# Expert weights over two DMA queues: the second gate/up quad and the down quad of experts 6 to 27 begun by ScalarE

## The reference

```python
def clamped_swiglu(hgu):
    g, u = hgu[..., :D_EXPERT], hgu[..., D_EXPERT:]
    g = jnp.minimum(g, SWIGLU_LIMIT)
    u = jnp.clip(u, -SWIGLU_LIMIT, SWIGLU_LIMIT)
    return (u + 1.0) * (g * jax.nn.sigmoid(SWIGLU_ALPHA * g))
...
    def expert_block(args):
        tok, e = args
        xb = xn[tok]
        hact = clamped_swiglu(xb @ w_gate_up[e] + b_gate_up[e])
        return hact @ w_down[e] + b_down[e]
```

## Time and profile before

| | before |
|---|---|
| median of 3 runs | 1257.85 us (1256.84 to 1258.02) |
| the profiled execution | 1257.53 us |
| its span, from the first to the last instruction | 1255.7 us |
| PE busy | 1183.1 us (94%) |
| DVE busy | 478.8 us (38%) |
| ACT busy | 250.5 us (20%) |
| bytes moved | 461.49 MB, mean 368 GB/s |

### The profile page before, as it was taken

One profiled execution on the slowest core, in us unless ns is written; L12 is line 12 of the kernel. 1 busy time (PEld: TensorE's weight loads), 2 busy tenths in 40 slices (PEclk: granted clock), 3 DMA queues, 4 the chain that ended last, 5 costly groups with the idle time before them and its releaser, 6 DMA issues.

```text
span 1255.7 us, 18113 instructions
## 1 busy us (share of the span) xinstructions
PE 1183.1 (94%) x7504; PEld 612.6 (49%) x7504; DVE 478.8 (38%) x741; ACT 250.5 (20%) x353; POOL 5.4 (0%) x12
## 2 busy tenths in 40 slices
PE   8999999999899999999999989999999999989997
PEld 7999998998533333333333333333333333333332
DVE  6867867654422332222222322222222222222223
ACT  5439544544400000000100010000000000001002
POOL 0000100000000000000000000000000000000000
PEclk9999999999999999999999999999999999999999
DMA  8525647644999999999999999999999999999995
GB/s 329 197 101 201 243 169 268 237 165 185 384 361 428 430 426 435 432 432 428 428 432 433 434 434 433 428 428 432 433 434 434 433 428 428 432 428 428 426 428 230
DMA packets 27341, 461.49 MB, mean 368 GB/s; under 512 B 3216, under 2 KB 3360, under 8 KB 4512
## 3 DMA queue, kind: packets, MB, share of 16 engines
q1 hardware_dynamic: 26784, 460.16, 87.5%
q0 software_dynamic: 224, 0.54, 0.2%
q10 hardware_dynamic: 288, 0.12, 0.0%
HBM read 459.76 MB, written 1.05 MB: 367 GB/s over the span
## 4 chain that ended last, share of the span: by engine, by line
PE 61%; DMA 37%; DVE 1%; issue 1%; ACT 0%; SPq 0%; DVEq 0%; ACTq 0%
DMA late<-in_w_gate_up 36%; PE ps L1370 29%; PE ps L1235 6%; PE ps L1236 6%; PE ps L1237 6%; PE ps L1419 3%; PE ps L1254 2%; PE ps L1255 2%; PE ps L1256 2%; PE ps L1270 2%; PE ps L1393 1%; PE ps L1427 1%; DMA raw<-in_dense 1%; PE ps L1323 1%; PE ps L1303 1%
## 5 line engine op out<-in xcount | busy, mean ns | idle before, releaser
L1370 PE MATMUL ps<-late,s 128*64 128x512 f32 x1224 | 556.4, 598 | 55.2 <-DMA late<-in_w_gate_up 53.9
L1371 PE MATMUL ps<-late,s 128*64 128x512 f32 x1224 | 556.4, 598 | 0.0
L1370 PEld LDWEIGHTS ps<-late,s 128*64 128x64 f32 x1224 | 155.7, 136 | 395.4 <-issue 304.0
L1119 DVE TENSOR_TENSOR res<-res,ps 128x1024 f32<-128x1024 f32 x64 | 78.1, 1221 | 246.2 <-PE ps L1419 238.8
L1235 PE MATMUL ps<-act_hi,whi 128*128 128x256 f32 x576 | 164.2, 285 | 3.5 <-DVE act_lo L776 1.8
L1237 PE MATMUL ps<-act_hi,wlo 128*128 128x256 f32 x576 | 163.7, 284 | 0.0
L1236 PE MATMUL ps<-act_lo,whi 128*128 128x256 f32 x576 | 163.7, 284 | 0.0
L1371 PEld LDWEIGHTS ps<-late,s 128*64 128x64 f32 x1224 | 155.7, 136 | 0.0
L692 ACT ACTIVATE early<-ps 128x512 f32<-128x512 f32 x64 | 34.7, 594 | 551.4 <-PE ps L1371 551.4
L795 DVE TENSOR_TENSOR wlo<-raw,whi 128x2048 fp32r<-128x2048 f32 x47 | 107.3, 2288 | 51.9 <-ACT whi L525 51.8
L1371 PE MATMUL ps<-raw,s 128*64 128x512 f32 x272 | 123.9, 598 | 0.0
(11 more groups left out here) (195 smaller groups left out, 876.9 us busy)
## 6 DMA issues: line engine op xcount, KB each, us to landing
late<-in_w_gate_up SPq DMA_DIRECT2D x44, 4096.0 KB, 21.0
late<-in_w_gate_up SPq DMA_DIRECT2D x31, 2048.0 KB, 15.7
raw<-in_dense SPq DMA_DIRECT2D x51, 1024.0 KB, 4.8
late<-in_w_down SPq DMA_DIRECT2D x11, 4096.0 KB, 20.6
raw<-in_w_down SPq DMA_DIRECT2D x11, 4096.0 KB, 20.6
late<-in_w_down SPq DMA_DIRECT2D x12, 2048.0 KB, 17.9
raw<-in_w_down SPq DMA_DIRECT2D x7, 2048.0 KB, 20.4
early<-in_w_gate_up SPq DMA_DIRECT2D x5, 2048.0 KB, 9.3
```

The lines of the kernel that those rows point to most:

```text
L1119: V.tensor_tensor(res[:, t, :], res[:, t, :], ps[:, OUT_BANK[t]:OUT_BANK[t] + 2, :].rearrange("p b n -> p (b n)"), ALU.add)\
L1370: nc.tensor.matmul(ps[0:SLOTS, bank, :], x_tile, lower, start=start, stop=stop)
L1371: return nc.tensor.matmul(ps[SLOTS:P, bank, :], x_tile, upper, start=start, stop=stop)
```

## The change

SP keeps the first gate/up quad of each expert from 6 to 27. The second gate/up quad and the down quad are begun by ACT on its own queue. The second quad of e+1 is begun after ACT's two copies of the gate/up rows in the step of e, the down quad of e at the start of ACT's work in the step of e, ahead of the copy of the down rows. The counts of `chunk_used` that are waited for are the same as on SP. ACT's loop over the experts is cut in three (1 to 5, 6 to 27 by twos, 28 to 31), with a branch that leaves out the second quad after expert 27. Before expert 6 and from expert 28 on, all weights stay on SP's queue.

```diff
-            def load_gate_up_quad(e, q):
-                sp.dma_start(flat[QUADS[q]], gate_rows(e, q)).then_inc(filled[QUADS[q]], 16)
...
-            def load_down_quad(i, half):
-                at = QUADS[2 + half]
-                sp.dma_start(flat[at], down_rows(i * 2 + half)).then_inc(filled[at], 16)
...
-                def next_gate_up_quads(e):
-                    for q in range(2):
-                        used(r, e, 4 * q + 3)
-                        load_gate_up_quad(e + 1, q)
-
-                with sp.Fori(QUAD_FROM // 2 - 1, QUAD_UNTIL // 2 - 1) as i:
-                    for half in range(2):
-                        e = i * 2 + (1 + half)
-                        next_gate_up_quads(e)
-                        used(r, e, PER_EXPERT - 1)
-                        load_down_quad(i + 1, half)
+                with sp.Fori(QUAD_FROM - 1, QUAD_UNTIL - 1) as e:
+                    used(r, e, 3)
+                    sp.dma_start(flat[QUADS[0]], gate_rows(e + 1, 0)).then_inc(filled[QUADS[0]], 16)
                 next_gate_up(QUAD_UNTIL - 1)
...
+            def load_second_gates(r, e):
+                act.wait_ge(S["chunk_used"], number(r, e, GU_CHUNKS))
+                act.dma_start(flat[QUADS[1]], w_gate_up[bass.ds((e + 1) * (D // 4) + P, P), :])\
+                    .then_inc(filled[QUADS[1]], 16)
+
+            def load_downs(r, e, half):
+                act.wait_ge(S["chunk_used"], number(r, e, 0))
+                act.dma_start(flat[QUADS[2 + half]], w_down[bass.ds(e * P, P), :]).then_inc(filled[QUADS[2 + half]], 16)
+
             n = needed_rounds(act)
             with act.Fori(0, n) as r:
                 rows_out(r, 0, PER_EXPERT)
-                with act.Fori(1, EXPERTS) as e:
-                    rows_copied(r, e)
+
+                def between(r, e):
                     gate_sigmoid(r * EXPERTS + e)
                     rows_out(r, e, GU_CHUNKS)
+
+                with act.Fori(1, QUAD_FROM) as e:
+                    rows_copied(r, e)
+                    between(r, e)
+                load_second_gates(r, QUAD_FROM - 1)
+                with act.Fori(QUAD_FROM // 2, QUAD_UNTIL // 2) as i:
+                    for half in range(2):
+                        e = i * 2 + half
+                        load_downs(r, e, half)
+                        rows_copied(r, e)
+                        between(r, e)
+                        if half == 0:
+                            load_second_gates(r, e)
+                        else:
+                            with act.If(i < QUAD_UNTIL // 2 - 1):
+                                load_second_gates(r, e)
+                with act.Fori(QUAD_UNTIL, EXPERTS) as e:
+                    rows_copied(r, e)
+                    between(r, e)
```

## The result

The changed kernel takes 1261.24 us (median of 12 runs, 1259.99 to 1263.92), the kernel before 1257.51 us (12 runs beside them). The ratio is 1.0029, with an interval from 1.0022 to 1.0037: slower by 2.8 to 4.7 us, beyond the 0.2% (2.5 us) up to which the forecast counted "the same". The forecast was 1259.8 us and "the same"; its range, 1256.0 to 1263.5, holds the result. The profiled execution took 1261.55 us, its span is 1259.8 us, 4.1 us longer than before.

A forecast was written before the change was run, and what follows sets the result against it. Memory was taken as the bound, with PE waiting twice a step. To the 1257.5 us before, only 2.3 us were added, a 4.2 us late first quad of expert 27 less 1.9 us of existing wait: 1259.8 us, range 1256.0 to 1263.5.

The forecast's parts named there:

- The bound: Expert loop: memory sets the 29.14 us step at 432 GB/s; PE's own work is 2.48 us shorter and waits twice.
- Issues and waits on ACT at nothing: ACT's two issues a step, 0.5 us each, and its already-needed waits cost nothing; without cover the issues would be 22 us.
- Shares: Memory engines: each queue gets half while both have work, so a 9.72 us quad takes 19.44; chance 0.55 with the drift.
- turns by whole transfers: Rival: engines finish their share of one transfer before the other queue's, so landings stay and time is 1257.5 us; chance 0.17.
- The drift of 3.9 to 4.5 us, and 2.3 us of it at the end: First gate/up quad lands 0.4 us later each step until the drift ends; 2.3 us lengthen the time.
- ACT's queue running dry: Limit of the drift: after 3.5 to 4.1 us SP's quad briefly has the engines alone and regains its 0.4 us.
- 4.2 - 1.9 = 2.3 us remain on the chain of PE: Expert 27: first quad lands 4.2 us late, PE's 1.91 us wait before chunk five absorbs part, 2.3 us remain.
- No order of transfers at this rate lands that quad sooner: Expert 27's second gate/up quad: at 1113.46 engines had moved exactly what PE used, so no gain below 1257.5 us.
- A higher pace: Rival: a second queue works in gaps at the pieces' edges, saving up to 6.6 us, 1251 to 1257 us; chance 0.11.
- A cost of changing queues: Rival: each queue change costs the engines up to 0.56 us, 22 us in all, 1261 to 1280 us; chance 0.13.
- ACT late or fetching code: Rival: ACT's longer loop fetches instruction blocks at 0.1 to 0.56 us each, up to 11 us, 1269 us; chance 0.04.
- The rival "slower": Whole kernel: time above 1260.4 us, chance 0.33, from the drift's upper part 0.16, queue changes 0.13 and ACT 0.04.

The follow-up runs named there:

- the spare matmuls: Changed kernel plus 14 matmuls with unused results on PE ahead of the first chunk of experts 8, 10 to 26: 1260.1 us, ratio 1.0021.
- the run with both mended: Changed kernel with experts 26 and 27 begun by SP again and 14 unused matmuls before every second expert's first chunk: 1258.21 us, ratio 1.0009.

## Why the prediction was right or wrong

**The bound.** Right: memory sets the pace, and the two settled steps of 58.29 us at 432 GB/s show it. The change can only move the time by what happens at the end, or by bytes not moved.

**Issues and waits on ACT at nothing.** Right in the loop: with all three quads on ACT the settled steps and waits are those of before. An issue holds ACT for 0.34 us, where 0.5 were taken.

**Shares.** Right. In the stretch 594 to 613 of the kernel after, SP's first quad and ACT's quads are moved at 436 GB/s; below it is its begin, 594 to 598 (queue, packets, MB, share of the engines):

```profile
q1 hardware_dynamic: 144, 4.19, 51.1%
q10 hardware_dynamic: 141, 4.10, 49.9%
...
DMA packets 57, 1.87 MB, mean 467 GB/s; under 512 B 0, under 2 KB 0, under 8 KB 0
q10 hardware_dynamic: 29, 0.95, 55.0%
q1 hardware_dynamic: 28, 0.92, 53.1%
```

The first quad took 22.2 us where 21.74 were forecast; but only every second one shares like this, and the next took 15.9. The first two rows alone would fit turns by whole transfers too, since 144 packets are just one quad. The stretch 594 to 598 refutes these: from 592 to 594 all pieces are still ACT's, and no small packet, with which an engine ends its share, falls between 592 and 598; yet both queues then move large pieces, 28 and 29 of them, on the 16 engines. So the trace disagrees with the rule of the Trainium skill, DMA: Bandwidth & Descriptors, section Queues, rings and completion order, if a quad's nine pieces on an engine are one packet.

**The drift of 3.9 to 4.5 us, and 2.3 us of it at the end.** The size was right where the clock doesn't fall: 4.04 us later at the first chunk of expert 27, +2.06 at the fifth (1115.52; the forecast said near 1116). Taking the last two experts back to SP gave 1.9 us of the time back. The way to it was wrong, and so its size is in part luck. The forecast had 0.4 us more with every step, over ten steps. But with the spare matmuls expert 9, the fourth on two queues, is 4.00 us late already (582.38 against this row of before), and expert 27 is 4.04:

```profile
578.38 0.64 PE L1370 MATMUL ps<-late,s 128*64 128x512 f32 x1 [1.55 <-DMA late<-in_w_gate_up]
```

The limit it reasoned from, ACT's queue running dry, is in the trace: from 623 to 635 in the kernel after, SP's quad has 76.0% of the engines and ACT's 24.1%. (Its own figures give 600.2 - 588.5 = 11.7 us for a distance that it took as 10.4 to 11.5; this moves the drift by under 0.1 us.) The form was wrong too: the forecast had 2.5 us of idleness before the first chunk of every step, and it came as 3.4 to 4.3 us before every second one. What makes the steps go in pairs stays open. They go on without the lowered clock, since at 1.00 the restarts of experts 26 and 27 are 27.92 us apart, where a mean step has 29.14; expert 26 is 5.26 us late, expert 27 4.04. The run meant to tell (the second quad of expert 6 on SP) did not.

**What the sum lacked.** The step that failed is "4.2 - 1.9 = 2.3 us remain on the chain of PE": a late first quad does set the end, but its size was off, 4.2 where 6.07 was measured. In the kernel after the first chunk of expert 27 starts 6.07 us later (1108.95 against 1102.88), and 4.03 remain at the fifth. The sum took PE's work per step as fixed, whatever the size of its idleness. Few long waits in place of many short ones let the clock fall. At the last of them this put the issue of the next quad 2.88 us later. Of the 2.03 us by which the spare matmuls bring expert 27 forward (1106.92 for 1108.95), 0.64 are there at expert 26 (1079.00 for 1079.64) and 1.39 come in this last step. In all they gave back 0.9 us (by the table) to 2.0 us (spans 1259.8 and 1257.8); the times alone don't show it clear of noise. That carried the time across the bound from "the same", forecast at 0.56, to "slower", at 0.33. What remains in the run with both mended, +0.93 us with an interval from 0 to 2.3, is not explained; the long wait left in its trace may be part of it.

**"No order of transfers at this rate lands that quad sooner."** Wrong as an argument: with the down quads behind it, it landed some 6 us sooner. The bound of no gain held for another reason: the engines then ran short, and PE waited later.

**The other rivals.** A higher pace: not seen, 430 to 433 GB/s; the Trainium skill, DMA: Bandwidth & Descriptors, section Rules for kernel authors, has it that spreading over issuing engines doesn't help bandwidth, and the trace agrees. A cost of changing queues: not there, since the pieces of two queues are mixed at 436 GB/s in 594 to 613 and the settled pair of steps runs at 432. ACT late or fetching code: not seen, the third queue has 37 packets in both kernels. The rival "slower" came true by a mechanism that none of them named.

**Of what was to be seen:** the split of the bytes by one to two is there (184.67 MB on ACT, so 92 of SP's). The down quads were to take longer than 20.6 us, which was wrong: the one begun at 610.12 landed after 18.9.

## What to carry to other kernels

When the memory is the bound and one queue is always full, a second queue brings no pace, but lets a transfer that isn't urgent take half the engines from one that PE waits for; look which transfer is needed next before giving others their own queue. Moving a transfer that "has room" later in the line is no gain either, if it is what the engines live on meanwhile. And a sum of waits isn't enough: see whether they are many short or few long ones, as the latter can cost PE its clock.

## What the runs showed of the hardware

In the kernel after the engines alternate between two queues with large pieces at no cost: 51.1% and 49.9% of the time at 436 GB/s (594 to 613). PE's granted clock fell to 0.50 (1.2 GHz) behind an idleness of 4.02 us in an otherwise busy stream (1079.64), and chunk-long stretches then run with matmuls of 1.06 us in place of 0.59; with all quads on ACT it fell behind 2.27 us as well. Matmuls on data already there, put into the idleness, kept it at 1.00. The Trainium skill, TensorE: Matmul & The Clock Gate, section What's actually happening, says that the throttled state is the default and activity releases it; both the fall and the 1.00 agree.
